# Expert outputs scattered to rows of their tokens, and the last stage reading plain rows instead of gathering them

## What is computed

```python
A = T * MOE_TOPK                      # 512 * 8 = 4096 assignments, number token * 8 + j
...
_, top_e = lax.top_k(jnp.where(emask, choice, -jnp.inf), MOE_TOPK)
gw = jnp.take_along_axis(scores, top_e, axis=1)
gw = gw / jnp.sum(gw, axis=-1, keepdims=True) * ROUTED_SCALE
...
def step(y, blk):
    tok, wt, e = blk
    out = swiglu(hf[tok], exp_gate[e], exp_up[e], exp_down[e])
    return y.at[tok].add(out.astype(F32) * wt[:, None]), None
...
shared = swiglu(hf, sh_gate, sh_up, sh_down)
return (y.astype(h.dtype) + shared).reshape(B, S, D)
...
x = x + g2 * moe_ffn(h2, ...)
return rms_norm_2(x, final_g)
```

## Time and profile before

| | |
|---|---|
| time, median of three runs (lowest, highest) | 2345.62 us (2340.84, 2349.48) |
| span of the profiled execution | 2343.3 us |
| TensorE busy | 2151.4 us, 92% |
| VectorE, ScalarE, GpSimd busy | 1330.6, 461.2, 396.7 us |
| read from DRAM, written to it | 416.27 MB, 73.45 MB |
| expert stage | about 1666 to 2269 us |
| combine stage | 2269 us to the end |

### The profile page before, as it was taken

The page is one execution under the profiler, slowest core; times in us unless marked ns, Lnnn a source line. Parts: engine busy times, 40 slices in busy tenths (PEclk is TensorE's granted clock), DMA queues, the critical chain, the costliest instruction groups (busy, mean ns, idle before and its releaser), DMA issues. The chain is left out here.

```text
span 2343.3 us, 27600 instructions
## 1 busy us (share of the span) xinstructions
PE 2151.4 (92%) x10395; PEld 1246.3 (53%) x10395; DVE 1330.6 (57%) x2524; ACT 461.2 (20%) x916; POOL 396.7 (17%) x771
## 2 busy tenths in 40 slices
PE   6999989999999999999879999998699999999975
PEld 3444554777785458883443788445333333333322
DVE  3448863766672134434968333535766766767745
ACT  2013561121120011004235232011011111111111
POOL 0005000111000000000000000000444444444433
PEclk9999999999999999999989999998799999999988
DMA  9422000535524015981111100401499999898976
GB/s 389 180 81 81 36 1 20 233 144 216 215 81 179 36 72 229 391 306 54 37 57 58 51 3 4 177 36 54 180 372 397 425 353 421 344 407 357 413 281 252
DMA packets 68999, 446.60 MB, mean 191 GB/s; under 512 B 12276, under 2 KB 12932, under 8 KB 44066
## 3 DMA queue, kind: packets, MB, share of 16 engines
q0 software_dynamic: 36176, 254.42, 27.1%
q1 hardware_dynamic: 32722, 190.78, 21.0%
HBM read 416.27 MB, written 73.45 MB: 209 GB/s over the span
## 5 line engine op out<-in xcount | busy, mean ns | idle before, releaser
L965 PE MATMUL psum<-arena 128*128 128x256 f32 x1904 | 416.7, 381 | 2.1 <-PEq L1005 2.0
L2824 PE MATMUL psum<-arena 128*64 128x512 f32 (+1 forms) x1088 | 366.1, 600 | 38.9 <-DVE arena L2872 16.6
L965 PEld LDWEIGHTS psum<-arena 128*128 128x128 f32 x1904 | 361.4, 190 | 62.6 <-issue 14.0
L2872 DVE STREAM_TRANSPOSE arena<-arena 32x256 f32<-32x256 f32 x832 | 362.1, 435 | 15.8 <-DMA arena<-scratch_h,arena 4.1
L2824 PEld LDWEIGHTS psum<-arena 128*64 128x64 f32 (+1 forms) x1088 | 143.8, 165 | 226.6 <-issue 197.7
L2815 PE MATMUL psum<-arena 128*64 128x512 f32 (+1 forms) x544 | 186.2, 598 | 1.2 <-ACT arena L2850 1.2
L1067 PE MATMUL psum<-arena 128*128 128x512 f32 x352 | 151.8, 592 | 0.3 <-PEq L1091 0.3
L2815 PEld LDWEIGHTS psum<-arena 128*64 128x64 f32 (+1 forms) x544 | 68.5, 163 | 113.2 <-issue 111.8
L869 PE MATMUL psum<-arena 128*128 128x512 f32 x256 | 111.2, 593 | 2.3 <-DVE arena L2432 1.5
L1067 PEld LDWEIGHTS psum<-arena 128*128 128x128 f32 x352 | 66.6, 190 | 83.4 <-issue 83.4
L2878 DVE COPY arena<-psum 128x512 f32<-128x512 f32 x51 | 35.3, 692 | 132.7 <-PE psum L2815 132.7
(11 more groups left out here) (521 smaller groups left out, 2932.0 us busy)
## 6 DMA issues: line engine op xcount, KB each, us to landing
scratch_expert_out<-arena SPq DMA_DIRECT2D x18, 2048.0 KB, 19.9
scratch_expert_out<-arena SPq DMA_DIRECT2D x51, 512.0 KB, 9.9
arena<-in_w_ada SPq DMA_DIRECT2D x12, 2048.0 KB, 16.8
arena<-in_ada_w POOLq DMA_DIRECT2D x12, 2048.0 KB, 8.8
arena<-in_w_up SPq DMA_DIRECT2D x22, 1024.0 KB, 4.8
arena<-in_w_in SPq DMA_DIRECT2D x9, 2048.0 KB, 11.0
arena<-in_w_down SPq DMA_DIRECT2D x5, 2048.0 KB, 8.6
arena<-in_w_o SPq DMA_DIRECT2D x2, 2048.0 KB, 8.4
```

Source lines behind the costliest of these rows:

```text
L965: last = pe.matmul(out, w[:, k, :], x[:, k, :], start=(k == 0), stop=(k == KH - 1))
L2824: last = pe.matmul(K.bank[2 + s][r, :], xt[:, s, P * k + r.start:P * k + r.stop], gu[:, lane, 2 * E_FF * k:2 * E_FF * (k + 1)], start=(k = ...
L2872: last = dve.transpose(channels[c:c + 32, :, a:a + 32], tokens[a:a + 32, :, c:c + 32])
```

## The change

Each assignment gets a row of its own in `expert_out`, number token x 8 + j; the buffer becomes 4096 rows of 1024 numbers. The one-hot products of `phase_route` now carry the assignment number; `K.asg` keeps it, and `K.tok` is that number shifted right by three. In `phase_experts` SyncE has no work; on GpSimd each step ends with the scatter of the block four back (`LAG`): it waits for the two copies of that block, copies the row numbers, waits for that, does a small add, and issues an indirect DMA from `out` to `expert_out`, in which rows out of bounds are skipped. The last four scatters follow the last step. In `phase_combine` GpSimd has no work; SyncE loads per tile the rows of 128 tokens, three rows of each for VectorE and five of each for TensorE, in two DMAs, into a ring of two tiles; tiles 0 and 1 at once, then the gate row and the norm's row, and tiles 2 and 3 as the buffers come free. The fill in `phase_in2` is gone.

```diff
@@ phase_in2
-    filled = sig("expert_out_filled")
...
-            def fill(count):
-                for _ in range(count):
-                    n = parts.pop(0)
-                    filled.by(sp.dma_start(d["expert_out"][n:n + NT].rearrange("b p n -> p b n"), K.res[:, :, :]), 16)
-
             for n in range(2, 7):
                 stream(K, sp, d["w_in2"][n])
-                fill(3)
...
-            fill(len(parts))
-            sp.wait_ge(filled.sem, filled.n)
@@ phase_route
-                    last = ts(place[:, t, j, :], count[:, 0:BLOCKS], part[:, 1, n:n + 1], const[:, RC_TOKEN + t:RC_TOKEN + t + 1], ALU.is_equal, ALU.mult)
+                    last = ts(place[:, t, j, :], count[:, 0:BLOCKS], part[:, 1, n:n + 1], const[:, RC_TOKEN + n:RC_TOKEN + n + 1], ALU.is_equal, ALU.mult)
...
-            step(ts(K.tok[:, 0:BLOCKS], K.bank[4][:, 0:BLOCKS], 2.0 * T, None, ALU.add))
+            step(ts(K.asg[:, 0:BLOCKS], K.bank[4][:, 0:BLOCKS], 2.0 * T * TOP, None, ALU.add))
+            step(ts(K.tok[:, 0:BLOCKS], K.asg[:, 0:BLOCKS], TOP.bit_length() - 1, None, ALU.logical_shift_right))
@@ phase_experts
-    U = UNROLL
+    U, LAG = UNROLL, 4
...
+            def scatter(i, s, off):
+                b = (s + off) % U
+                blocks_done(pool, out_act, i, s, off)
+                blocks_done(pool, out_dve, i, s, off)
+                pool.tensor_copy(out_rows[:, b:b + 1], K.asg[:, at(i, s + off)]).then_inc(out_step.sem, 1)
+                blocks_done(pool, out_step, i, s, off)
+                pool.tensor_tensor(wait_for[:, 6:7], K.rstd[:, 0:1], K.rstd[:, 0:1], ALU.add)
+                pool.indirect_dma_start(d["expert_out"], bass.IndirectOffsetOnAxis(ap=out_rows[:, b:b + 1], axis=0), out[:, b, :], None,
+                                        bounds_check=T * TOP - 1, oob_is_err=False).then_inc(out_dma[b].sem, 16)
...
                     gather(i, s, 1)
                     weights(i, s)
-
-            steps(pool, step)
+                if not isinstance(i, int) or U * i + s >= LAG:
+                    scatter(i, s, -LAG)
+
+            def rest(n):
+                for off in range(-LAG, 0):
+                    scatter(n, U, off)
+
+            steps(pool, step, rest)
 
         @block.sync
         def _(sp):
-            def step(i, s):
-                blocks_done(sp, out_act, i, s, 0)
-                blocks_done(sp, out_dve, i, s, 0)
-                dst = d["expert_out"][at(i, s)].rearrange("a p n -> (a p) n")
-                sp.dma_start(dst, out[:, s, :]).then_inc(out_dma[s].sem, 16)
-
-            steps(sp, step)
+            pass
@@ phase_combine
-    RING, ON_DVE = 16, 3
+    RING, ON_DVE = 2, 3
...
-            for n in range(NT * TOP):
-                if n >= RING:
-                    pool.wait_ge((summed if on_pe(n - RING) else used).sem, mine(n - RING))
-                sem_in[n % RING].by(pool.indirect_dma_start(yg[:, n % RING, :], None, d["expert_out"].rearrange("b p n -> (b p) n"),
-                                                            bass.IndirectOffsetOnAxis(ap=K.slot[:, n:n + 1], axis=0)), 16)
...
+            def load(t):
+                rows = d["expert_out"][P * TOP * t:P * TOP * (t + 1)].rearrange("(p j) n -> p j n", j=TOP)
+                if t >= RING:
+                    sp.wait_ge(used.sem, ON_DVE * (t - RING + 1))
+                dve_in[t % RING].by(sp.dma_start(yg[:, t % RING, 0:ON_DVE, :], rows[:, 0:ON_DVE, :]), 16)
+                if t >= RING:
+                    sp.wait_ge(summed.sem, ON_PE * (t - RING + 1))
+                pe_in[t % RING].by(sp.dma_start(yg[:, t % RING, ON_DVE:TOP, :], rows[:, ON_DVE:TOP, :]), 16)
+
+            for t in range(RING):
+                load(t)
             row_in.by(sp.dma_start(gate_row[:, :], d["mod_rows"][3].partition_broadcast(P)), 16)
             row_in.by(sp.dma_start(frow[:, :], d["rows"][ROWS.index("final_g_2")].partition_broadcast(P)), 16)
+            for t in range(2, NT):
+                load(t)
```

More of the change, by code:

```diff
@@ L1468, in _ @@
         def _(sp):
-            parts = [LANE * lane + t for lane in range(UNROLL) for t in range(8, LANE, NT)]
-            def fill(count):
-                for _ in range(count):
-                    n = parts.pop(0)
-                    filled.by(sp.dma_start(d["expert_out"][n:n + NT].rearrange("b p n -> p b n"), K.res[:, :, :]), 16)
             for n in range(2, 7):
                 stream(K, sp, d["w_in2"][n])
-                fill(3)
             stream(K, sp, d["w_v2"])
@@ L2458 @@
 NOWHERE = 1.0e6
-RC_LOWER, RC_TOKEN, RC_LANE, RC_TRIP, RC_ROW, RC_TWOS, RC_EXPERT, RC_COUNT, RC_N = 0, 64, 68, 69, 70, 71, 103, 167, 295
+RC_LOWER, RC_TOKEN, RC_LANE, RC_TRIP, RC_ROW, RC_TWOS, RC_EXPERT, RC_COUNT, RC_N = 0, 64, 96, 97, 98, 99, 131, 195, 323
 def phase_route(nc, K, ctx):
@@ L2469, in phase_route @@
     K.tok = sb("block_tokens", [P, BLOCKS + 8]).bitcast(U32)
+    K.asg = sb("block_assignments", [P, BLOCKS + 8]).bitcast(U32)
     K.source = sb("lane_sources", [P, LANES * LANE]).bitcast(U32)
@@ L2744, in phase_experts @@
     rows, wrows = sb("e_rows", [P, 8]).bitcast(U32), sb("e_weight_rows", [P, 8]).bitcast(U32)
+    out_rows = sb("e_out_rows", [P, 8]).bitcast(U32)
     wait_for = sb("e_wait_for", [P, 8])
+    out_step = sig("e_out_rows_ready")
     row_step, cleared = sig("e_rows_ready"), sig("e_x_cleared")
@@ L2957, in phase_combine @@
     ON_PE = TOP - ON_DVE
-    yg, out, gated = sb("c_rows", [P, RING, D]), sb("c_out", [P, NT, D]), sb("c_gated", [P, D])
+    yg, out, gated = sb("c_rows", [P, RING, TOP, D]), sb("c_out", [P, NT, D]), sb("c_gated", [P, D])
     frow, gate_row = sb("final_row", [P, D]), sb("gate_row", [P, D])
     diag = sb("c_diagonals", [P, NT, ON_PE, P])
-    sem_in = [K.dma_signal(f"c_landed{n}") for n in range(RING)]
+    dve_in, pe_in = ([K.dma_signal(f"{n}{r}") for r in range(RING)] for n in ("c_first_rows_landed", "c_last_rows_landed"))
@@ L2962, in phase_combine @@
     row_in, used, x3, squared, ms, root, done, stored = (sig(n) for n in ("final_landed", "c_used", "x3", "x3_squared", "x3_ms", "x3_root", "out_ready", "out_stored"))
     diag_in, summed, first = sig("c_diagonal_ready"), sig("c_summed"), sig("c_sum_read")
-    on_pe = lambda n: n % TOP >= ON_DVE
-    mine = lambda n: len([m for m in range(n + 1) if on_pe(m) == on_pe(n)])
     banks = lambda t: K.psum[:, D * (t % 2):D * (t % 2) + D]
     with nc.Block() as block:
-        @block.gpsimd
-        def _(pool):
-            for n in range(NT * TOP):
-                if n >= RING:
-                    pool.wait_ge((summed if on_pe(n - RING) else used).sem, mine(n - RING))
-                sem_in[n % RING].by(pool.indirect_dma_start(yg[:, n % RING, :], None, d["expert_out"].rearrange("b p n -> (b p) n"),
-                                                            bass.IndirectOffsetOnAxis(ap=K.slot[:, n:n + 1], axis=0)), 16)
@@ L2982, in _ @@
                 for j in range(ON_PE):
-                    n = TOP * t + ON_DVE + j
                     pe.wait_ge(diag_in.sem, ON_PE * t + j + 1)
-                    pe.wait_ge(sem_in[n % RING].sem, 16 * (n // RING + 1))
+                    if j == 0:
+                        pe.wait_ge(pe_in[t % RING].sem, 16 * (t // RING + 1))
                     for half in range(2):
-                        last = pe.matmul(banks(t)[:, 512 * half:512 * half + 512], diag[:, t, j, :], yg[:, n % RING, 512 * half:512 * half + 512],
+                        last = pe.matmul(banks(t)[:, 512 * half:512 * half + 512], diag[:, t, j, :], yg[:, t % RING, ON_DVE + j, 512 * half:512 * half + 512],
                                          start=(j == 0), stop=(j == ON_PE - 1))
@@ L2995, in _ @@
                 for j in range(ON_DVE):
-                    n = TOP * t + j
-                    dve.wait_ge(sem_in[n % RING].sem, 16 * (n // RING + 1))
-                    if j:
+                    if j == 0:
+                        dve.wait_ge(dve_in[t % RING].sem, 16 * (t // RING + 1))
+                    else:
                         dve.wait_ge(used.sem, used.n)
-                    used.by(dve.scalar_tensor_tensor(out=s, in0=yg[:, n % RING, :], scalar=K.weight[:, t, j:j + 1], in1=s, op0=ALU.mult, op1=ALU.add))
+                    used.by(dve.scalar_tensor_tensor(out=s, in0=yg[:, t % RING, j, :], scalar=K.weight[:, t, j:j + 1], in1=s, op0=ALU.mult, op1=ALU.add))
                 dve.wait_ge(used.sem, used.n)
@@ L3056, in build @@
     return K
[L3060 removed]
+SCRATCH = {"gate_rows": (2, 2 * KD, P), "toe_line": (HEADS, TOE), "toe_wide": (P * HEADS * TOE + P,), "mod_rows": (4, D), "gate_r": (P, KD, T), "h2": (T, D), "expert_out": (T * TOP, D)}
 def _columns(v):
```

5 lines of the change are left out of this document (2 added, 3 removed).

## The result

The changed kernel takes 2350.35 us (median of 18 runs, 2340.33 to 2354.73), the kernel before 2344.74 us in 18 runs beside it (2340.84 to 2349.48). The ratio is 1.002 with a 95% interval of 1.0012 to 1.0027, so 2.8 to 6.3 us slower. The forecast was 3.0 us faster. The time lies inside the wide range of 2326 to 2357 us and 0.35 us above the forecast's own of 2334 to 2350; the sign was wrong.

The account below looks back on a forecast made before the run. TensorE was taken to bound the expert stage, waiting almost only for gate-up weights. Fill 0, routing +0.3, expert stage -1.4, its end +1.7 and final stage -3.6 sum to -3.0 us: 2342.6 us, range 2334 to 2350 (wide 2326 to 2357).

Parts of the forecast that it names:

- The final stage: Combine stage: VectorE's 7.39 us wait goes, tile 3's late load then limits; -3.6 us, bounds -7.4 and +2.2.
- rival B: Combine stage: VectorE's 7.39 us wait comes back, +2.2 instead of -3.6 us; 2348.4 us, chance 0.13.
- The end of the expert stage: After the last copies: the scatter's issue replaces the quicker store issue, +1.7 us, bounds 0 and +9.0.
- The expert stage inside: Expert stage: later gate-up loads (+12.6) against saved bytes (-14.0), -1.4 us, bounds -14.0 and +12.6.
- the late gate-up load: Expert stage: the scatter delays it 2.1 us, paid at six stretch starts, +12.6 us.
- the bytes: Expert stage: unused rows no longer stored, 0.46 us saved for each of 31 blocks, -14.0 us.
- The clock's fall within the expert stage: Expert stage: TensorE's clock falling after a longer wait, listed as a sign of a wrong forecast; no size given.
- Rival C: Expert stage: issue order sets gate-up landings, all 18 waits grow by 2.1 us, +37.8; 2381.8 us, chance 0.08.
- D: Expert stage: VectorE slows GpSimd's descriptors, scatters 1 us longer, +6 us; 2348.6 us, chance 0.04.
- E: Expert stage: unused rows cost as much as used ones, +12.6 instead of -1.4 us; 2356.6 us, chance 0.05.
- F: Fill of the expert buffer: it costs time no wait shows, removal gives back 20.5 us; 2322.1 us, chance 0.03.
- A: Expert stage: the late issue is covered and saved bytes count fully, -14.0 instead of -1.4 us; 2330.0 us, chance 0.17.

Follow-up runs that it names:

- the runs of all rows: Changed kernel with every scatter moving all 128 rows of its block: 2355.86 us with the scatter behind the down load, 2344.09 us with it ahead.
- the run with the late issue alone: Kernel before, its plain stores kept, plus an indirect store on GpSimd behind each down load that moves no rows: 2366.29 us.

## Why the prediction was wrong

**The final stage** is the step that failed, and not in what it said of the changed kernel: counted from SyncE's first load, it put VectorE's first sum at 23.65 us, its second at 36.75 and its last at 60.35; the trace has 23.44, 35.92 and 60.64. What failed is the other side of the subtraction: "The sum of tile 1, at 2311.26 now". The wait of 7.39 us ahead of it was in one trace of four. The usual final stage lasts 63.8 us, so the same step, rightly sized, is +2.7 (most of it tile 3's late rows, 2.3 to 3.0 us at the last sum in three traces of four) and not -3.6. That the sums came so near their forecast is partly luck: TensorE could start on tile 0 1.0 us earlier than said, but took 11.1 us instead of 10.3; the second sum was early by 0.8, but the half clock cost the last tile's products 2.5 us (11.32 instead of 8.82), where 1.5 was said. The warning stood in rival B: by the same timeline TensorE had ended 10 us before the sum that was said to wait for it. B itself didn't come about, as the changed kernel's second sum waits for nothing in any trace; that its 2348.4 us lies near the measured time is chance. That profiled execution as a whole looked like the median, since its early stages were 3.5 to 5.5 us quicker than in the other traces.

**The end of the expert stage**: the landing was right (+1.7, measured +1.63; it lands 4.50 us after the last copy, where 4.5 was said). The barrier behind it, +1.4 us, was not in the sum: a store moved to GpSimd makes the stage wait for GpSimd to finish, too.

**The expert stage inside**: the late gate-up load is 2.09 us later, as said, and +12.6 was the forecast for it; the runs give 11.8 to 13.4, of which 7.7 to 10.3 are waits. Part of the rest is steps run at the lower clock, for which the sum has no term here, so that the size fits partly by luck. The term mis-sized is the bytes, -14.0: the unused rows gave 5.5 us in the change's place (one trace against four), and the store's move to GpSimd, for which the sum has no term, 7.0. That these two together come near 14.0 is luck as well; +0.9 came instead of -1.4.

**Right**: the fill cost nothing, as the stage that held it lasts 188.6 us with it and without; the routing; waits of 22.4 us at the gate-up line (19.5 to 23.4 in the four traces); ScalarE never waits at its copies for a scatter. The clock's fall within the expert stage, named as a sign of being wrong, came, but it is in three of the four traces of before, too. Rival C (every wait grows) fell with the waits, D with scatters of 1.03 us: the port rule that the Trainium skill states in "SBUF — State Buffer", "SBUF: two separate sides", shows in none of the 51 (1.04 us at most). E fell with the runs of all rows, F with the unchanged stage of the fill. A came about only where the issue is not late: there the stage is 11.9 us shorter than before's.

**The sum by the runs**: 0.2 + 0.9 + 1.6 + 1.4 and, for the final stage, +1.0 against the mean of all four traces of before make +5.1 us, inside the measured 2.8 to 6.3. Against the usual final stage (+2.7) it is +6.8, 0.5 us beyond the interval; how often the odd final stage comes in runs that aren't traced is not known. The forecast held that less than 11.7 us can't be told from no change; with 18 runs of each kernel 2.8 to 6.3 us could.

## What to carry to other kernels

Trace the kernel twice before subtracting from it: a wait whose named cause ended long ago may belong to the execution, and a total near the median can hide two odd stages of opposite sign. In an engine's queue, put a new issue where that engine waits anyway and not ahead of what refills a queue that has run dry: here this alone was worth 13 us. In a stage that VectorE's chain bounds, loads matter only up to the first sum, and then for whatever stands last in their queue.

## What was not expected of the hardware

The stage that ends on GpSimd's indirect store starts its successor 1.86 us after the last wait for a landing is over; with SyncE's plain store it was 0.45 us.

TensorE's granted clock fell to 0.5 (1.2 of 2.4 GHz) in the middle of the expert stage, behind a wait of 2.58 us, the longest of the changed kernel; that step took 8.83 us, where other steps of this form behind a wait took 7.13. TensorE's timeline and two stretches of the changed kernel (columns as in the earlier trace rows):

```profile
1757.93 8.83 PE L2817 MATMUL psum<-arena 128*128 128x512 f32 x16 [2.58 <-DMA arena<-in_exp_gu,arena]
```

```profile
1759.00:1762.00 3.00, 3.00 (x5) 1.20 (x4) 2.92 (x7) 0.00 (x0) 2.29 (x8) 0.50 1.09 448
1763.00:1766.00 3.00, 3.00 (x8) 1.33 (x7) 0.00 (x0) 0.00 (x0) 1.78 (x2) 1.00 0.96 407
```

That wait so cost 1.7 us more than its own length. The second trace of the changed kernel has the same fall at the same place. It is no price of the change alone, as the second, third and fourth trace of before have one such fall each. Nor does the wait's length decide it: in the first trace of before no fall followed 2.46 us, and in the run with the late issue alone none followed 2.83 us, but one followed 1.90:

```profile
1892.26 7.09 PE L2826 MATMUL psum<-arena 128*64 128x512 f32 x32 [2.83 <-issue]
...
2146.01 8.83 PE L2826 MATMUL psum<-arena 128*128 128x512 f32 x16 [1.90 <-DMA arena<-in_exp_gu,arena]
```
